# Last block of a three-part network: the low parts of 25 weight blocks made by accumulating transfers instead of a VectorE subtraction

## The reference

```python
mod = silu(c) @ ada_w + ada_b
shift, scale, gate = split(mod, 3)
h = rmsnorm(x, norm_g) * (1 + scale) + shift
p = h @ w_in                                   # [256, 9344]
c_val, c_gate, c_og, ts, r_og, g_conv, g_rwkv = split(p)
u = c_val * sigmoid(c_gate)
u = causal_depthwise_conv(u, conv_k, width 31) + conv_b
y_conv = (silu(layernorm(u)) * silu(c_og)) @ w_conv_out
r, k, v, w_low, a_low = split(token_shift(ts))
o = rwkv7_scan(...)                            # 16 heads, state 64 x 64
y_rwkv = ((groupnorm(o) + bonus) * silu(r_og)) @ w_rwkv_out
x = x + gate * ((sigmoid(g_conv)*y_conv + sigmoid(g_rwkv)*y_rwkv) @ w_out)
out = rmsnorm(x, final_g)
```

## Time and profile before

| | |
|---|---|
| time before, median of 3 | 1036.64 us |
| the profiled execution's own time | 1036.78 us |
| its span on the core | 1035.0 us |
| the steps' starts (line 2762 of each pair, DVE) | step -1 641.9, 0 679.3, 1 717.6, 2 757.4, 3 795.1, 4 834.6, 5 869.0, 6 901.1 us |
| low halves of 128 x 1024 (line 304) | 86, of which 50 in steps -2 to 4 |

### The profile page before, as it was taken

How to read it: one execution, slowest core, us unless ns; L and a number is a source line. 1 busy time by engine, 2 the same in 40 slices (tenths; PEclk the granted TensorE clock), 3 DMA queues, 4 the chain that set the end, 5 groups by cost and what they waited for, 6 DMA issues and landing times.

```text
span 1035.0 us, 25000 instructions
## 1 busy us (share of the span) xinstructions
PE 1002.3 (97%) x10690; PEld 932.6 (90%) x10690; DVE 869.7 (84%) x1447; ACT 604.3 (58%) x875; POOL 18.4 (2%) x38
## 2 busy tenths in 40 slices
PE   7999999999999999999999999999999999899997
PEld 6999999999999989989898998889999998789996
DVE  7866699899988886999899897989999999965474
ACT  7755664444446756554444577556657676686443
POOL 2000000000000000000000000000000000000000
PEclk9999999999999999999999999999999999999999
DMA  9662457777554515576775646334323422234531
GB/s 283 214 203 94 152 189 252 230 243 227 199 176 149 164 47 181 200 231 227 241 234 182 203 133 194 109 99 124 122 86 123 125 84 84 84 124 155 170 126 41
DMA packets 136075, 168.26 MB, mean 163 GB/s; under 512 B 3216, under 2 KB 125328, under 8 KB 135728
## 3 DMA queue, kind: packets, MB, share of 16 engines
q1 hardware_dynamic: 132080, 153.44, 46.1%
q0 software_dynamic: 3904, 13.50, 4.0%
HBM read 164.83 MB, written 2.10 MB: 161 GB/s over the span
## 4 chain that ended last, share of the span: by engine, by line
PE 68%; DVE 22%; ACT 6%; issue 2%; DMA 2%; SPq 0%; DVEq 0%; ACTq 0%
PE banks L353 13%; PE banks L318 8%; PE banks L319 7%; PE banks L320 7%; PE banks L355 7%; DVE hf L2652 4%; DVE w_parts L304 3%; DVE w_parts L280 3%; PE banks L655 2%; PE bank L657 2%; PE bank L655 2%; PE banks L657 2%; PE bank L659 2%; PE banks L659 2%; ACT w_parts L275 1%
## 5 line engine op out<-in xcount | busy, mean ns | idle before, releaser
L280 DVE TENSOR_TENSOR w_parts<-raw,w_parts 128x2048 fp32r<-128x2048 f32 x95 | 217.1, 2288 | 27.3 <-ACT w_parts L275 26.8
L353 PE MATMUL banks<-x_parts,w_parts 128*128 128x512 f32 x640 | 227.1, 399 | 0.0
L318 PE MATMUL banks<-x_parts,w_parts 128*128 128x256 f32 x704 | 211.9, 301 | 0.0
L319 PE MATMUL banks<-x_parts,w_parts 128*128 128x256 f32 x736 | 208.3, 283 | 0.0
L320 PE MATMUL banks<-x_parts,w_parts 128*128 128x256 f32 x704 | 199.1, 283 | 0.0
L275 ACT ACTIVATE w_parts<-raw 128x2048 fp32r<-128x2048 f32 x95 | 180.9, 1905 | 3.6 <-PE banks L810 2.1
L355 PE MATMUL banks<-x_parts,w_parts 128*128 128x256 f32 x640 | 179.8, 281 | 0.0
L353 PEld LDWEIGHTS banks<-x_parts,w_parts 128*128 128x128 f32 x640 | 120.3, 188 | 29.0
L319 PEld LDWEIGHTS banks<-x_parts,w_parts 128*128 128x128 f32 x736 | 141.2, 192 | 0.5 <-issue 0.5
L318 PEld LDWEIGHTS banks<-x_parts,w_parts 128*128 128x128 f32 x704 | 134.5, 191 | 7.6 <-issue 0.7
L320 PEld LDWEIGHTS banks<-x_parts,w_parts 128*128 128x128 f32 x704 | 134.8, 192 | 0.0
(11 more groups left out here) (418 smaller groups left out, 2411.6 us busy)
## 6 DMA issues: line engine op xcount, KB each, us to landing
raw<-in_ffn_w_up SPq DMA_DIRECT2D x44, 1024.0 KB, 5.1
raw<-in_w_in SPq DMA_DIRECT2D x36, 1024.0 KB, 5.5
raw<-in_ffn_w_down SPq DMA_DIRECT2D x22, 1024.0 KB, 5.9
big<-in_ada_w_t POOLq DMA_DIRECT2D x24, 512.0 KB, 4.1
raw<-in_gla_w_in SPq DMA_DIRECT2D x11, 1024.0 KB, 5.6
raw<-in_attn_w_qkv SPq DMA_DIRECT2D x6, 1024.0 KB, 4.9
raw<-in_gla_w_out SPq DMA_DIRECT2D x4, 1024.0 KB, 5.5
raw<-in_attn_w_out SPq DMA_DIRECT2D x4, 1024.0 KB, 4.9
```

The costliest lines, as they stand in the source:

```text
L280: eng.tensor_tensor(WL[:, n % RING, :, :], RAW[:, n % RING, :, :], WH[:, n % RING, :, :].bitcast(F32), ALU.subtract).then_inc(w_lo_ready, 1)
L318: nc.tensor.matmul(ps, wh, xh, start=start, stop=False)
L319: nc.tensor.matmul(ps, wh, xl, start=False, stop=False)
L353: nc.tensor.matmul(PS[bank + m].rearrange("p (a t) -> p a t", a=2), WH[:, s, k, ms], XP[:, :, k, :], start=k == 0, stop=False, skip_group_ ...
```

## The change

For the 25 blocks from r1 to gc2 the low part is made in another way. DVE no longer reads RAW: it writes the negative of the high part into WL (`minus_hi_half`, a tensor_scalar with the constant -1.0, same 128 x 1024 halves, same places in its order). POOL then issues a transfer from RAW (SBUF) to WL (SBUF) with an add, for each half, waits for both to land, and adds one to `w_lo_ready` itself (`raw_added`). PE, and SP's load of block n + 3, wait for the same semaphore as before, but the one who raises it is now POOL, after the landing. Behind the 25 blocks DVE goes back to subtracting, and before its first half there (of rog3) it waits until the last of the 25 is complete. The remaining lines of the diff give several events of the layer norm and of the small low-rank product one semaphore in common with higher counts (`ln_on_dve`, `ln_on_act`, `lora_on_act`), which waits for the same events.

```diff
+N_ADD, N_ADD_END = PLACE["r", 1], PLACE["gc", 2] + 1
...
         def split_lo_half(dve, n, half):
             if half == 0:
                 dve.wait_ge(w_hi_ready, n + 1)
+                if n == N_ADD_END:
+                    dve.wait_ge(w_lo_ready, n)
...
+        def minus_hi_half(dve, n, half):
+            if half == 0:
+                dve.wait_ge(w_hi_ready, n + 1)
+            ks = slice(4 * half, 4 * half + 4)
+            dve.tensor_scalar(WL[:, n % RING, ks, :], WH[:, n % RING, ks, :].bitcast(F32), -1.0, None, ALU.mult)\
+                .then_inc(sem("minus_hi"), 1)
+
+        def raw_added(pool, n):
+            if n == N_ADD:
+                pool.wait_ge(w_lo_ready, n)
+            for half in range(2):
+                ks = slice(4 * half, 4 * half + 4)
+                pool.wait_ge(sem("minus_hi"), 2 * (n - N_ADD) + half + 1)
+                pool.dma_start(WL[:, n % RING, ks, :].bitcast(F32), RAW[:, n % RING, ks, :], accum_op=ALU.add)\
+                    .then_inc(sem("raw_added"), 16)
+            pool.wait_ge(sem("raw_added"), 32 * (n - N_ADD + 1))
+            pool.sem_inc(w_lo_ready, 1)
...
+            for n in range(N_ADD, N_ADD_END):
+                raw_added(pool, n)
...
-                        put_at(s, q, ("hi" if u < 4 else "lo", n + 2, u // 2 % 2))
+                        lo = "minus_hi" if N_ADD <= n + 2 < N_ADD_END else "lo"
+                        put_at(s, q, ("hi" if u < 4 else lo, n + 2, u // 2 % 2))
...
-                    pe.wait_ge(sem("conv_done"), 1)
+                    pe.wait_ge(sem("ln_on_dve"), 1)
...
-            nc.scalar.activation(WLH, w_lora, ACT.Copy).then_inc(sem("lora_hi"), 1)
+            nc.scalar.activation(WLH, w_lora, ACT.Copy).then_inc(sem("lora_on_act"), 1)
```

More of the change, by code:

```diff
@@ L1089, in ln @@
                 if step == 3:
-                    pe.wait_ge(sem("ln_steps"), 2)
+                    pe.wait_ge(sem("ln_on_dve"), 3)
                     for m in range(2):
@@ L1107, in pre_activations @@
             def pre_activations(p):
-                pe.wait_ge(sem("lora_ready"), 1)
+                pe.wait_ge(sem("lora_on_act"), 3)
                 if p:
@@ L1150, in gn_sums @@
                     if p >= 5:
-                        pe.wait_ge(sem("ln_rstd"), 1)
+                        pe.wait_ge(sem("ln_on_act"), 2)
                     pe.wait_ge(sem("gn_squares"), p + 1)
@@ L1824, in _ @@
             act.wait_ge(sem("lora_rows"), 1)
-            nc.scalar.activation(Z, PS[3][:, 0:T], ACT.Copy).then_inc(sem("lora_taken"), 1)
+            nc.scalar.activation(Z, PS[3][:, 0:T], ACT.Copy).then_inc(sem("lora_on_act"), 1)
             split_hi(act, N_L3 + 4)
             act.wait_ge(sem("lora_steps"), 2)
-            nc.scalar.activation(LORA[0:64, :], LORA[0:64, :], ACT.Tanh).then_inc(sem("lora_ready"), 1)
+            nc.scalar.activation(LORA[0:64, :], LORA[0:64, :], ACT.Tanh).then_inc(sem("lora_on_act"), 1)
             def split_hi_whole(n):
@@ L1885, in ln @@
                 if step == 2:
-                    act.wait_ge(sem("ln_steps"), 1)
-                    nc.scalar.activation(S8, CONV, ACT.Square).then_inc(sem("ln_squares"), 1)
+                    act.wait_ge(sem("ln_on_dve"), 2)
+                    nc.scalar.activation(S8, CONV, ACT.Square).then_inc(sem("ln_on_act"), 1)
                 if step == 4:
@@ L1890, in ln @@
                     act.wait_ge(sem("ln_sums"), 2)
-                    rsqrt(LNR, PS[2][:, 0:T], 1.0 / D, eps_ln, "ln_rstd")
+                    rsqrt(LNR, PS[2][:, 0:T], 1.0 / D, eps_ln, "ln_on_act")
                 if step == 6:
-                    act.wait_ge(sem("conv_normed"), 1)
+                    act.wait_ge(sem("ln_on_dve"), 4)
                     table("silu")
@@ L1896, in ln @@
                         ins = nc.scalar.activation(CONV[:, g, :], CONV[:, g, :], ACT.Silu, bias=vec("conv_ln_b_2", g))
-                    ins.then_inc(sem("conv_silu"), 1)
+                    ins.then_inc(sem("ln_on_act"), 1)
             def slot(s, r):
@@ L2574, in _ @@
             scaled(0)
-            dve.wait_ge(sem("lora_hi"), 1)
+            dve.wait_ge(sem("lora_on_act"), 1)
             v.tensor_tensor(WLL, w_lora, WLH.bitcast(F32), ALU.subtract).then_inc(sem("lora_steps"), 1)
@@ L2588, in _ @@
             lo(N_L3 + 3)
-            dve.wait_ge(sem("lora_taken"), 1)
+            dve.wait_ge(sem("lora_on_act"), 2)
             v.tensor_tensor(LORA[:, 1:T], Z[:, 0:T - 1], Z[:, 1:T], ALU.subtract)
@@ L2622, in use_block @@
                     if j == 0:
-                        dve.wait_ge(sem("conv_silu"), 1)
+                        dve.wait_ge(sem("ln_on_act"), 3)
                     v.tensor_tensor(CONV[:, js, :], CONV[:, js, :], GT[:, j % 2, :, :], ALU.mult)\
@@ L2657, in taps @@
                     ch.all()
-                    v.tensor_tensor(CSUM, CSUM, CONV[:, 6:8, :], ALU.add).then_inc(sem("conv_done"), 1)
+                    v.tensor_tensor(CSUM, CSUM, CONV[:, 6:8, :], ALU.add).then_inc(sem("ln_on_dve"), 1)
             def three_pairs_added():
@@ L2671, in ln @@
                                                      ALU.mult, ALU.add)
-                    ins.then_inc(sem("ln_steps"), 1)
+                    ins.then_inc(sem("ln_on_dve"), 1)
                 if step == 3:
-                    dve.wait_ge(sem("ln_squares"), 1)
+                    dve.wait_ge(sem("ln_on_act"), 1)
                     ch.step(v.tensor_tensor(S8[:, 0:4, :], S8[:, 0:4, :], S8[:, 4:8, :], ALU.add))
                     v.tensor_tensor(S8[:, 0:2, :], S8[:, 0:2, :], S8[:, 2:4, :], ALU.add)\
-                        .then_inc(sem("ln_steps"), 1)
+                        .then_inc(sem("ln_on_dve"), 1)
                 if step == 5:
-                    dve.wait_ge(sem("ln_rstd"), 1)
+                    dve.wait_ge(sem("ln_on_act"), 2)
                     for g in range(KT):
@@ L2682, in ln @@
                                                      ALU.mult, ALU.mult)
-                    ins.then_inc(sem("conv_normed"), 1)
+                    ins.then_inc(sem("ln_on_dve"), 1)
             def slot(s, r):
@@ L2688, in slot @@
                         split_lo_half(dve, item[1], item[2])
+                    elif item[0] == "minus_hi":
+                        minus_hi_half(nc.vector, item[1], item[2])
                     elif item[0] == "use":
```

## The result

The change made the kernel slower: 1085.34 us median (1084.67 to 1085.81) against 1036.58 us, ratio 1.0471 with a 95% interval of 1.0452 to 1.0489. The first of the three rivals, transfers that land late, is what happened.

The account below looks back on a forecast made before the run. PE and DVE were both taken as almost full, so relief on DVE returns only PE's waits: 0.5 + 2.1 + 1.5 + 1.0 + 1.1 + 0.5 = 6.7, taken as 7, 1036.6 - 7 = 1029.6 us; range 1027.5 to 1046.

Parts of the forecast that it names:

- 0.69 forecast: On DVE, the negation of a 1024-column half takes 0.69 us, 0.53 us less than the subtraction.
- the waits summed to 6.7: PE's waits for DVE in steps -2 to 5, with small gaps, would shrink by 6.7 us, taken as 7.
- 0.5 forecast: Step -2: half of PE's 1.1 us wait goes, as the operands also wait for ACT's exponentials: 0.5 us.
- small gaps: Gaps below 0.3 us where a block ends and DVE's result just comes in time: 0.5 us, by judgement.
- I take 6 us for a half and a load of the engines of 0.8, which hides it: POOL's adding transfer lands 6 us after issue and the DMA engines are 0.8 full, so transfers cost nothing.
- lead of 9.2 us: Tightest block, gate2: 9.2 us from DVE's shortened second half to PE's use, the limit for a landing.
- the 9.6 us of a block: A block's time, within which the DMA engines must fit load and adds: 6.5 us, or 9.7 at half rate.
- Rival 1: Transfers land late, past 9.2 us, or 9.6 per block; PE waits at each block's first matmul; slower; chance 0.29.
- its 12 us case: If landings take 12 us: 56 us lost less 7 gained, some 1085 us.
- the range ended at 1046: Overall range 1027.5 to 1046 us, its end from late transfers at 10 us; some 0.8 chance in all.
- a lead of ten units: Each half is made ten units of 1.2 us before PE uses it; 1 us more asks 0.8 us per block.
- The new wait before rog3: DVE's wait for the last landing before rog3's subtraction: 8.7 us of room; if it bites, PE is held behind it.

Follow-up runs that it names:

- e1: The change without its adding transfers, VectorE raising `w_lo_ready` itself and not waiting before rog3: 1028.47 us.
- e7: The change with the loads of the 25 blocks behind the first ones cut to one eighth of each block: 1028.86 us.
- e4: The change with PE and SP waiting for landings directly, a semaphore per slot, no landing wait on POOL, none on VectorE before rog3: 1032.33 us.
- e9: As e4, but POOL waits for each block's two halves to land before going on to the next: 1085.57 us.
- e2: The change with plain copies instead of adds, so the low parts are the raw weights; all waits stay: 1035.23 us.
- e10: The change with POOL's loop kept for 25 blocks but its own semaphore raised, so VectorE needs no wait before rog3: 1080.77 us.
- e8: As e4, but only 13 chosen blocks made by transfers, those before VectorE results that PE was waiting for: 1033.20 us.
- e12: As e4, but only nine chosen blocks made by transfers, where VectorE holds PE up longest: 1033.28 us.
- e5: As e4, but only every second of the 25 blocks, 13 in all, made by transfers, the others subtracted: 1032.24 us.

## Why the prediction was wrong

**Right: what VectorE gains.** The negation takes 683 ns (0.69 forecast) and writes the rounded format at the faster rate. VectorE's waiting lines in steps -2 to 4 vanish from PE's list, the 2.5 us of line 2783 in step 5 stay (they stand in e1's list with the same 2.5), and e1 gives 8.2 us where the waits summed to 6.7 and I took 7. The places fit too. By PE's first matmul of line 1170 in each step (line 1191 in e1), e1 gains 1.3 us up to step -1 (0.5 forecast), 2.1 in step -1 (2.1), 2.7 in steps 0 to 3 (1.5 and most of the 0.5 for small gaps), 1.1 in step 4 (1.0) and 1.1 in step 5 (1.1). Step -2 and the small gaps were worth more than I took.

**Wrong: "I take 6 us for a half and a load of the engines of 0.8, which hides it".** The 6 us was near for an add with an eighth of the load beside it (median 5.4 in e7) and too low beside a whole one (7.4 in e4), and the share of 0.8 was 0.94 in e4; neither miss alone makes a loss, as e4 shows. The step that failed is that I set a single transfer's latency beside the lead of 9.2 us and the engines' sum beside the 9.6 us of a block, as two separate tests. The change has a third: POOL takes up no block before the last has landed, so issue, load, adds and landing add up in one loop. The rows for that were there: 3.3 us of load and 6.4 of adding at half rate, and of the 4.1 us landing all but the 1.6 us of data is fixed, 2.5 us. With one issue of 0.5 us that is 12.7 us with the adds at half a copy's rate, and with the adds at a plain copy's rate still 9.5, on the edge. Measured: load 3.7, adds 5.0, landing 2.3, issue 0.9. The front part even said that "at most one block is under way", and I didn't price it. e9 shows that this wait alone makes the difference. e7 and e2 show that the loop needs both its load and its costly adds to be far over a block's time: with the load cut to an eighth it fits, with copies instead of adds it just about does.

**Wrong: the weight and the width.** Rival 1 named the mechanism (PE waits at each block's first matmul) and the threshold of 9.6 us, and its 12 us case gave 1085, by luck to the microsecond. But I gave it 0.29 and took 10 us for its likely size, so the range ended at 1046. Its own argument, 0.8 us more per block for each us of latency, wasn't what happened either; it rested on a lead of ten units, which at 1.2 us would be 12 us where the rows gave 9 to 11. The loop sets the pace: in steps -1 to 3 a block takes (874.99 - 640.46) / 20 = 11.7 us in the change (starts of line 2788) and (826.96 - 640.34) / 20 = 9.3 us in e7 (line 2792). From the start of step -1 to that of step 5 this makes 51.1 of the 56.5 us between the change and e7, and step 5, with VectorE's wait, 4.6 more.

**The new wait before rog3** bit as described, for 3.9 us, because POOL was late, not because one transfer was slow. e10 puts its price at 4.6 us, the same as step 5's share above.

**What an add and an issue cost.** The Trainium skill's page "Collectives: The Full Stack" (section "The bandwidth ceiling: the fold count and why AG ≠ RS ≠ AR") says of a collective's reduce that its add needs two reads, hence half the rate. The ratio here agrees: 85 engine-us per MB against 39 for a copy on the same path, 2.2 times. That the second read is the cause, no run shows. The page "SBUF — State Buffer" of the Trainium skill (section "SBUF: two separate sides") says that GpSimd can't write descriptors while VectorE is in a two-port mode. The traces agree (below): in e4 three of the 50 issues are 0.3 to 0.65 us longer, and in the change two pairs, at 711.18 and 782.01, take 2.17 and 2.28 us instead of 1.75. That is at most about 1 us of the loss, and e4, which has no such loss, has 1.5 us of it.

**Open.** Between no transfers (1028.5) and direct ones (1032.3) 3.8 us remain. In the profiled executions (1028.47 and 1032.67) the place can be read: by the same PE matmuls as above, e4 loses 1.4 us against e1 in step -1, 1.2 in step 0, 0.2 in steps 1 to 4 and 1.2 in step 5. The chain of work that ended last in steps -1 and 0 of e4 runs over transfers that are late (start, length, what):

```profile
639.06 12.92 DMA raw<-in_w_in
652.01 2.02 ACT w_parts L300 x2
...
658.98 8.79 DMA w_parts<-raw
...
695.78 9.79 DMA w_parts<-raw
```

The first is a load that takes 12.9 us, where the median in that run from 700 to 850 us is 8.2, and ScalarE waits 1.6 us for it. In e8 and e12 ScalarE waits for a late load in step -1 as well (1.6 and 2.3 us), in e1, e5 and e7 it doesn't. In step 5 e4 has 0.7 us and e12 2.1 us in which PE stands idle and nothing in the profile released it. So late loads behind the first adds are a part of it; the rest, and what step 5's gap is, stays open. The spread is open too: with adds and whole loads (e4, e5, e8, e12) single executions lie 2 to 5 us apart, in e1 and e7 (adds, but short loads) within 0.8. In e8 the clock goes with it: the three slower executions (1034.4 to 1035.4 us) have a mean granted clock of 0.994 to 0.995, the three faster (1030.3 to 1032.0) 0.996 to 0.998. In e4 it doesn't: all six read 0.996.

**The clock in the loss.** No run held TensorE's clock. From 700 to 850 us the mean granted clock is 0.93 in the change and 1.00 in e4. One of the stretches at half clock, 1.2 instead of 2.4 GHz, starts at 711.7 us, behind 2.3 us in which PE was busy for only 0.39. That costs PE time, but it can't have set the pace of the 25 blocks: POOL was released by its own landing in all 24 turns, and SP's loads by POOL, so with a full clock PE would have waited longer at the same loop. What it costs behind the loop no run shows.

## What to carry to other kernels

When an engine issues a transfer and waits for its landing before it takes up the next, add up everything in that circle (issue, what the same landing releases ahead of it, data, landing) and compare the sum with the period; each part may fit by itself and the loop still be late. Let the consumers wait for the landing, with a semaphore for each buffer slot, and the issuer only for its data: here that one wait was worth 53 us. Before moving work from an engine to transfers, run the version with the work simply left out: here its 8.2 us bound the gain, and the versions that still do all the work and were faster than before kept 3.4 to 4.4 of them (1036.71 less 1033.28, and 1036.68 less 1032.24).

## What the runs showed of the hardware that was not expected

- An add in SBUF takes the issuer 0.86 us (median in e4 and e7), a copy of the same size 0.53 us (median in e2).
- In the change the load and the adds take turns on the engines and don't mix. From 700.1 to 703.8 us the load's queue has 82.8% of the engines and the adds' 0.6%, though POOL had begun to issue the first add at 699.24; in the first pair, with no load about, packets came some 1.5 us after the issue began. Three more turns, from 712.0, 758.9 and 865.4 us, give the load 88 to 91% of such a stretch and the adds 11% at most.
- VectorE's negations and POOL's issues collide. Three issues of e4 are longer than 0.86 us by more than 0.1: 1.17 us at 636.39, 1.51 at 710.05 and 1.43 at 825.98. Each has a negation that starts within it and ends 0.08 to 0.10 us before it does. Beside the taps alone, which stand behind most of the negations, issues keep their 0.86. The longest (VectorE and POOL, about 710 us):

```profile
710.46 0.41 DVE L2675 TENSOR_SCALAR hf<-big,vecs 128x256 f32<-128x256 f32 x1
710.79 0.69 DVE L317 TENSOR_SCALAR w_parts<-w_parts 128x1024 fp32r<-128x1024 f32 x1
...
710.05 1.51 POOL L324 DMA_DIRECT2D w_parts<-raw  x1 [5.06 <-DVE w_parts L317]
```
